# Narrower matmuls in the block solve of a hybrid layer's recurrence, and ten weight k-steps moved out of it

## The chip, the cores and the metric

The kernel runs on one core of one Trainium2 chip. The time is the device time of one execution in microseconds (us); of several runs the median is taken, and less is better. TensorE (PE in the profile) does the matmuls, and its weight loads have rows of their own (PEld). VectorE is DVE, ScalarE is ACT, GpSimd is POOL, SyncE is SP.

## The reference, cut to what matters

The layer is a chain of three blocks over 256 tokens. The change touches one branch of the first: a two-directional recurrence with 12 heads of 64 channels.

```python
def rwkv7_scan(r, w, k, v, kk, a):
    decay = jnp.exp(-jnp.exp(w))
    b = kk * a
    def step(S, inp):
        r_t, d_t, k_t, v_t, kk_t, b_t = inp
        sa = jnp.einsum('bhij,bhj->bhi', S, -kk_t)
        S = S * d_t[:, :, None, :] + sa[..., None] * b_t[:, :, None, :] + v_t[..., None] * k_t[:, :, None, :]
        return S, jnp.einsum('bhij,bhj->bhi', S, r_t)
...
    for d in range(N_DIR):
...
        if d == 0:
            y_sum = y_sum + rwkv7_scan(r4, wd4, kd4, v4, kk, ad4)
        else:
            y_sum = y_sum + flip(rwkv7_scan(flip(r4), flip(wd4), flip(kd4), flip(v4), flip(kk), flip(ad4)))
```

Everything around it (projections, attention, two more blocks with wide feed-forward products) is dense matmul over a stream of weights.

## The kernel before, in words

**Weights.** One stream of 563 weight tiles of 2048x128 passes through the core. Each tile is two units of 8 k-steps. SP fetches a unit into `raw`, ACT makes its high part (`split_hi`, L325, 128x1024), DVE its low part (`split_lo`, L334, 128x1024), and TensorE does three matmuls for each k-step (`product`, L345 to L347: high by high, high by low, low by high, 256 moving columns). The order of work on every engine is the order of the code; engines meet through counting semaphores (`need` waits for a named step of another engine, L199).

**The recurrence** is done in 4 chunks of 64 tokens (`NCH`, `CH`), for 6 pairs of heads (`PAIRS`), both directions `d` = 0 and 1 together. `pe_rwkv` is written out for the 6 pairs; on the other engines a pair is one round of a loop. Each pair has on TensorE: projections and a transpose, three groups of products of the chunk's keys (the grams: `mt`, `kat`, `m`, then `brt`, `krt`, `btok`, then `katv`, `krtv`, `ktok` and `u0_1`), a block solve in levels, and four steps through the chunks. A product is 8 matmuls of 64x64 by 64 columns (4 chunks, 2 heads); in float32 each has two records in the trace. Direction 1 crosses the heads (`cross`), so that the two directions use different quarters of the array, and `both` takes two products in turns.

**The levels** invert a triangular matrix per chunk: at level `l` (1 to 5) blocks of 2^l rows are joined in twos. For each direction, `level_x` multiplies `tm` by the masked matrix `ml[l]` into a bank, ACT copies the result to `x` (L1211), `level_t` and `level_u` multiply it with `u`, and DVE adds the banks to `tm` (L1292) and `u` (L1300). `tm` and `u` are the inverse and its transpose. TensorE takes the directions half a level apart: in one half step it does a double group (one direction's X, the other's T) and a single group (a U). All matmuls, copies and additions work on all 64 columns of each chunk.

**Weight k-steps among it.** Beside each pair 4 weight tiles are multiplied, 64 k-steps. `go(n)` puts the next n of them into TensorE's order: `GO_START` 2, `GO_PREP` 25, `GO_GRAM` 5, 4 and 6 behind the three grams, 10 among the levels (`GO_LEVEL`, two at first and one in each half step behind it), `GO_SOLVED` 2 behind the solve, and one (`GO_STEP`) at each of ten places of the chunk steps. The splits of later units stand in the levels too: on DVE `split_lo` behind the T addition of direction 1 in levels 1, 2 and 4, and a gate at level 3; on ACT `split_hi` behind levels 1 and 3. POOL makes `ml[l]` (L1152, L1163) and `u` from `mt` while the levels run.

Of the kernel before, what the change touches and what calls it, by code (L numbers as in the profile page):

```python
# [17 lines left out]
P = 128  # L18
D = 2048
KT = D // P  # L20
T = 256
# [70 lines left out]
GO_START, GO_PREP, GO_LEVEL, GO_SOLVED, GO_STEP = 2, 25, 1, 2, 1  # L92
GO_GRAM = (5, 4, 6)
# [157 lines left out]
def build(nc, stream, consts, params, w2, a2, wgu, memT, xT, metaT, out):  # L251
# [4 lines left out]
    with ctx:  # L256
# [721 lines left out]
        for d in range(2):  # L978
            o = B + 82 * K + 20 * K * d
            w = {}  # L980

            for k, n in enumerate(("abd", "rbd", "bbd", "kbd", "mt", "tm", "brt", "btok", "ktok", "nkatv", "kat", "krt", "u", "x")):
# [49 lines left out]
        def dve_kk(v, u):  # L1032
# [7 lines left out]
            elif u == A_T + X_T - 1:  # L1040
                kk_v.done(nc.vector.tensor_scalar(hw_sb[:], par[:, PCOL["w0"]:PCOL["w0"] + 24], 0.5, None, ALU.mult), "half")
                need(v, kk_v, "inv2")
                for b in THIRDS:
                    for p in (2 * b, 2 * b + 1):
# [7 lines left out]
                     + [f"{n}{d}" for d in D2 for n in (("t1_", "ml1_", "u0_", "u1_") if d == 0 else ("t1_", "ml1_"))]  # L1052
                     + [f"ml2_{d}" for d in D2] + ["u1_1"] + [f"ml{l}_{d}" for l in LV if l > 2 for d in D2])
# [75 lines left out]

        def chunk_of(d, s):  # L1130
            return s if d == 0 else NCH - 1 - s

        def pool_rwkv(pool):
# [4 lines left out]
            with pool.Fori(0, PAIRS) as p:  # L1138
# [8 lines left out]
                ident = four(const("istack"))  # L1147
                for d, w in enumerate(dirs):

                    need(pool, rw_v, f"m{d}", p)  # L1150
                    rw_o.done(nc.gpsimd.tensor_tensor(w["tm"][:], w["tm"][:], ident, ALU.add), f"t1_{d}")
                    rw_o.done(nc.gpsimd.tensor_tensor(w["ml"][1][:], w["mt"][:], level(1), ALU.mult), f"ml1_{d}")  # L1152
                    if d == 0:
                        rw_o.done(nc.gpsimd.tensor_tensor(w["u"][:], w["mt"][:], level(0), ALU.mult), f"u0_{d}")
                        need(pool, rw_o, f"u0_{d}", p)
                        rw_o.done(nc.gpsimd.tensor_tensor(w["u"][:], w["u"][:], ident, ALU.add), f"u1_{d}")
                for l in LV:
                    if l > 1:
                        for d, w in enumerate(dirs):
                            if l == 2 and d == 0:  # L1160

                                need(pool, rw_v, "q", p)
                            rw_o.done(nc.gpsimd.tensor_tensor(w["ml"][l][:], w["mt"][:], level(l), ALU.mult), f"ml{l}_{d}")  # L1163
                    if l == 2:
# [8 lines left out]
        def act_rwkv(act):  # L1173
# [3 lines left out]
            with act.Fori(0, PAIRS) as p:  # L1177
# [47 lines left out]
        def dve_rwkv(v):  # L1225
# [4 lines left out]
            with v.Fori(0, PAIRS) as p:  # L1230
# [57 lines left out]
                for l in LV:  # L1288
                    for d, w in enumerate(dirs):
                        if l < LEVELS - 1:  # L1290
                            need(v, rw_p, f"T{l}_{d}", p)
                            rw_v.done(nc.vector.tensor_tensor(w["tm"][:], w["tm"][:], value_part(bank_of(d, 0), 0), ALU.add), f"T{l}_{d}")  # L1292
# [7 lines left out]
                        rw_v.done(nc.vector.tensor_tensor(w["u"][:], w["u"][:], value_part(bank_of(d, 2), 0), ALU.add), f"U{l}_{d}")  # L1300
# [38 lines left out]
        def pe_rwkv(pe):  # L1339
# [3 lines left out]
            for p in range(PAIRS):  # L1343
# [68 lines left out]
                def level_x(l, d):  # L1412
# [8 lines left out]
                    return bank_of(d, 1), 0, w["ml"][l], w["tm"], d, f"X{l}_{d}"  # L1421
# [11 lines left out]
                def level_t(l, d):  # L1433
                    level_known(l, d)
                    return bank_of(d, 0), 0, dirs[d]["u"], dirs[d]["x"], d, f"T{l}_{d}"

                def level_u(l, d):
                    level_known(l, d)
                    return bank_of(d, 2), 0, dirs[d]["x"], dirs[d]["u"], 0, f"U{l}_{d}"

                for l in LV:
# [5 lines left out]
                    go(2 * GO_LEVEL if l == 1 else GO_LEVEL)  # L1447
# [5 lines left out]
                    if l < LEVELS - 1:  # L1453
                        go(GO_LEVEL)
                both(level_u(LEVELS - 1, 1))
                go(GO_SOLVED)
                for s in ST:
# [39 lines left out]
                    go(GO_STEP if s < NCH - 1 else BESIDE * KT - GO_START - GO_PREP - sum(GO_GRAM) - 2 * (LEVELS - 1) * GO_LEVEL - GO_SOLVED - (3 * NCH - 2) * GO_STEP)  # L1497
# [1866 lines left out]
```

How the kernel before makes its waits and increments, by code:

```python
def need(eng, steps, name, it=None):  # L197
    eng.wait_ge(steps.sem, steps.at(name, it))
# [88 lines left out]
        def folded(v, phase, tile, bank):  # L288
            nc.vector.tensor_reduce(fold[tile.parity][:], bank[:].rearrange("p (a t) -> p t a", a=2), AX.X, ALU.add).then_inc(fold_out, 1)
            v.wait_ge(fold_out, tile.local(1, fold_done(phase, 1)))
            return fold[tile.parity][:]
# [5 lines left out]
        def halves_added(v, phase, tile, ins, dst, bank, out_sem):  # L298
            ins.then_inc(half_out, 1)
            v.wait_ge(half_out, tile.local(1, 1 + sum(COUNT[q] for q in HALVED[:HALVED.index(phase)])))
            nc.vector.tensor_tensor(dst, dst, bank[:, T:], ALU.add).then_inc(out_sem, 1)
# [12 lines left out]
        def split_hi(act, tile, units=(0, 1)):  # L315
            if not tile.loops and tile.first + tile.t >= N_TILES + PAD:
                return
            for k in units:
                slot = (2 * tile.parity + k) % RING
                g = tile.first + tile.t
                act.wait_ge(raw_in[slot], tile.sum(16 * (g // 2 + 1), 8))
                if not tile.start:
                    act.wait_ge(units_used, tile.units(k + 1 - RING))
                nc.scalar.activation(w_hi[:, slot], raw[:, slot], ACT.Copy).then_inc(hi_ready, 1)
# [1 line left out]
        def split_lo(v, tile, units=(0, 1)):  # L327
# [3 lines left out]
            for k in units:  # L331
                slot = (2 * tile.parity + k) % RING
                v.wait_ge(hi_ready, tile.units(k + 1))
                nc.vector.tensor_tensor(w_lo[:, slot], raw[:, slot], w_hi[:, slot].bitcast(F),
```

## Time and profile before

| | |
|---|---|
| median of 3 runs | 3526.99 us |
| lowest and highest | 3524.95 and 3529.78 us |
| the profiled execution, its own time | 3526.12 us |
| its span in the trace | 3524.0 us |
| mean granted TensorE clock | 0.995 of full speed |
| instructions in the trace | 75021 |

The span runs from the first to the last instruction of the profiled execution; its own time is 2.12 us more. In the views below, a matmul's row begins where it enters the array and its length is modelled, and rows of successive matmuls overlap: how fast they follow each other is read from the starts. "x16" is 16 records merged.

### The profile page before, as it was taken

Reading aid. Unit: us, or ns where it says so; the run is one execution under the profiler, and the core shown is the slowest. Engines: PE = TensorE matmul, PEld = TensorE weight load, DVE = VectorE, ACT = ScalarE, POOL = GpSimd, SP = SyncE. Lnnn points to the kernel's source line nnn. Section 1 sums busy time; section 2 is a strip of 40 time slices with the busy share of each in tenths; the row PEclk is TensorE's granted clock in tenths of the full one; section 3 lists DMA queues with packets and bytes.
Section 4 is the critical chain, followed back from the end, with each engine's and each line's share of the span. In section 5 each row is a group of like instructions: output and inputs, shape, how many; then the busy total and the mean of one; then the engine's idle time right before and its main releaser. Section 6 shows DMA issues by size and latency. Waiting matters only on the chain.

```text
span 3524.0 us, 75021 instructions
## 1 busy us (share of the span) xinstructions
PE 3456.2 (98%) x27870; PEld 3151.2 (89%) x27870; DVE 2423.2 (69%) x3490; ACT 1642.0 (47%) x2248; POOL 289.4 (8%) x358
## 2 busy tenths in 40 slices
PE   8999999999999999999999999999999999999998
PEld 8999888899988899999888888888899988888886
DVE  6986777755676677976756565677766865656566
ACT  6456334444444434754444444444444644434344
POOL 5000234200020000002000000020000200000002
PEclk9999999999999999999999999999999999999999
DMA  7444222255655555555565555555554555555564
GB/s 253 160 156 144 86 86 86 82 171 179 204 191 188 184 178 175 168 169 181 185 194 181 194 185 193 182 188 191 174 161 162 173 185 185 191 185 194 181 194 140
DMA packets 164985, 604.04 MB, mean 171 GB/s; under 512 B 18336, under 2 KB 18464, under 8 KB 164560
## 3 DMA queue, kind: packets, MB, share of 16 engines
q1 hardware_dynamic: 163584, 596.16, 51.8%
q8 instruction: 135, 2.21, 0.3%
q10 hardware_dynamic: 1040, 3.16, 0.2%
q0 software_dynamic: 192, 2.23, 0.2%
q14 instruction: 34, 0.28, 0.0%
HBM read 599.38 MB, written 2.10 MB: 171 GB/s over the span
## 4 chain that ended last, share of the span: by engine, by line
PE 90%; DVE 6%; ACT 2%; issue 1%; POOL 0%; DMA 0%; ACTq 0%; DVEq 0%; POOLq 0%
PE bank L366 35%; PE bank L369 18%; PE bank L345 11%; PE bank L346 10%; PE bank L347 10%; PE bank L1349 4%; DVE w_lo L334 2%; ACT w_hi L325 1%; POOL x_norm_acc L466 0%; DVE nrm_kk L1039 0%; DVE X L2900 0%; PE bank L848 0%; DVE X L2904 0%; PE bank L731 0%; DVE conv_sq L2584 0%
## 5 line engine op out<-in xcount | busy, mean ns | idle before, releaser
L325 ACT ACTIVATE w_hi<-raw 128x1024 fp32r<-128x1024 f32 x1126 | 1157.6, 1053 | 827.2 <-PE bank L369 510.5
L334 DVE TENSOR_TENSOR w_lo<-raw,w_hi 128x1024 fp32r<-128x1024 f32 x1126 | 1350.0, 1236 | 99.9 <-ACT w_hi L325 99.6
L366 PE MATMUL bank<-hid,w_hi 128*128 128x512 f32 x2048 | 643.4, 395 | 0.0
L366 PE MATMUL bank<-u,w_hi 128*128 128x512 f32 x1536 | 484.4, 397 | 0.0
L345 PE MATMUL bank<-hx,w_hi 128*128 128x256 f32 x1568 | 466.1, 297 | 12.1 <-DVE w_lo L334 12.1
L369 PEld LDWEIGHTS bank<-hid,w_lo 128*128 128x128 f32 x2048 | 384.7, 188 | 90.9
L346 PE MATMUL bank<-hx,w_hi 128*128 128x256 f32 x1568 | 445.3, 284 | 0.0
L347 PE MATMUL bank<-hx,w_lo 128*128 128x256 f32 x1568 | 444.9, 284 | 0.3 <-issue 0.3
L366 PE MATMUL bank<-xh,w_hi 128*128 128x512 f32 x1312 | 413.5, 397 | 2.7 <-DVE w_lo L334 2.7
L369 PE MATMUL bank<-hid,w_lo 128*128 128x256 f32 x2048 | 402.3, 278 | 0.0
L369 PEld LDWEIGHTS bank<-u,w_lo 128*128 128x128 f32 x1536 | 289.5, 189 | 69.2
L345 PEld LDWEIGHTS bank<-hx,w_hi 128*128 128x128 f32 x1568 | 302.1, 193 | 27.6 <-issue 16.8
L366 PEld LDWEIGHTS bank<-hid,w_hi 128*128 128x128 f32 x2048 | 311.8, 189 | 0.1
L346 PEld LDWEIGHTS bank<-hx,w_hi 128*128 128x128 f32 x1568 | 302.7, 193 | 1.0 <-issue 1.0
L369 PE MATMUL bank<-u,w_lo 128*128 128x256 f32 x1536 | 302.4, 278 | 0.0
L347 PEld LDWEIGHTS bank<-hx,w_lo 128*128 128x128 f32 x1568 | 302.3, 193 | 0.0
L369 PEld LDWEIGHTS bank<-xh,w_lo 128*128 128x128 f32 x1312 | 247.2, 188 | 58.5
L369 PE MATMUL bank<-xh,w_lo 128*128 128x256 f32 x1312 | 258.4, 278 | 0.0
L366 PEld LDWEIGHTS bank<-u,w_hi 128*128 128x128 f32 x1536 | 234.1, 188 | 0.1
L2308 DVE SCALAR_TENSOR_TENSOR X<-X,bank 128x256 f32 (+1 forms) x128 | 54.0, 422 | 256.6 <-PE bank L369 256.2
L345 PE MATMUL bank<-u,w_hi 128*128 128x272 f32 (+1 forms) x768 | 220.7, 287 | 6.0 <-DVE w_lo L334 6.0
L346 PE MATMUL bank<-u,w_hi 128*128 128x272 f32 (+1 forms) x768 | 220.7, 287 | 0.0
(477 smaller groups left out, 5559.3 us busy)
## 6 DMA issues: line engine op xcount, KB each, us to landing
raw<-stream SPq DMA_DIRECT2D x1126, 512.0 KB, 4.0
x_raw<-xT SPq DMA_DIRECT2D x4, 512.0 KB, 7.5
mem_raw<-memT ACTq DMA_DIRECT2D x4, 512.0 KB, 9.5
x_res<-xT POOLq DMA_DIRECT2D x1, 2048.0 KB, 9.7
out<-X SPq DMA_DIRECT2D x3, 512.0 KB, 2.7
cst<-consts SPq DMA_DIRECT2D x1, 1504.0 KB, 13.6
out<-X SPq DMA_DIRECT2D x2, 256.0 KB, 2.2
w_sb<-w ACTq DMA_DIRECT2D x1, 384.0 KB, 4.8
```

What stands on the lines that cost most here:

```text
L325: nc.scalar.activation(w_hi[:, slot], raw[:, slot], ACT.Copy).then_inc(hi_ready, 1)
L334: nc.vector.tensor_tensor(w_lo[:, slot], raw[:, slot], w_hi[:, slot].bitcast(F), ALU.subtract).then_inc(lo_ready, 1)
L345: nc.tensor.matmul(dst, w_hi[:, slot, j], hi, start=first, stop=False)
L346: nc.tensor.matmul(dst, w_hi[:, slot, j], lo, start=False, stop=False)
L347: return nc.tensor.matmul(dst, w_lo[:, slot, j], hi, start=False, stop=last)
L366: nc.tensor.matmul(bank[:], w_hi[:, slot, i], both(moving, kt), start=kt == 0, stop=False)
L369: last = nc.tensor.matmul(bank[:, T:], w_lo[:, slot, i], moving[:, kt, 0, moving.shape[-1] - T:], start=False, stop=kt == KT - 1)
L1349: last = nc.tensor.matmul(out[halves()[r ^ cross]], lhs[halves()[r]], rhs[halves()[r]], start=start, stop=stop)
L2308: nc.vector.scalar_tensor_tensor(self.x[:, m], self.x[:, m], self.scale if self.is_group(g, 0) else 1.0, banks[tile.parity][:, 0:T], ALU.m ...
```

## The change

Joining two blocks of 2^l rows changes only half of the columns. The changed kernel works on that half alone.

- `with_bit(ap, l, bit)` picks the columns whose number has bit l equal to `bit`: 32 of each chunk's 64, in runs of 2^l.
- X and T take and write the half with bit l equal to d, U the other half. Each of these matmuls has 32 moving columns in place of 64. What is loaded as weights (`ml[l]`, `u`, `x`) keeps its 64 columns, and so the number of matmuls and of loads stays.
- The copy on ACT and the two additions on DVE handle 128 elements a partition in place of 256.
- Since X serves as weights in full, its other half must be zero: POOL sets it, one memset for each level and direction (10 a pair), and each level has an `x` of its own, laid over tiles that are no longer needed (`kat`, `krt`, `kbd`, `bbd`). POOL waits for TensorE's `u0_1` before level 2, and ACT for the memset before each copy. ACT's wait for the U product of the level before is gone.
- The ten weight k-steps among the levels go: four more stand behind the second gram (`GO_GRAM` 5, 8, 8), two more behind the third, four more behind the solve (`GO_SOLVED` 6).

```diff
-GO_START, GO_PREP, GO_LEVEL, GO_SOLVED, GO_STEP = 2, 25, 1, 2, 1
-GO_GRAM = (5, 4, 6)
+GO_START, GO_PREP, GO_SOLVED, GO_STEP = 2, 25, 6, 1
+GO_GRAM = (5, 8, 8)
...
+            w["x"] = {l: at(f"x{l}_{d}", o + K * k, [P, NCH, CH]) for l, k in enumerate((13, 10, 11, 3, 2), 1)}
...
+        def with_bit(ap, l, bit):
+
+            if len(ap.shape) == 3:
+                ap = ap.rearrange("p c i -> p (c i)")
+            return ap.rearrange("p (g b t) -> p g b t", b=2, t=1 << l)[:, :, bit]
...
+                def rest_zero(l, d):
+                    rw_o.done(nc.gpsimd.memset(with_bit(dirs[d]["x"][l][:], l, 1 - d), 0.0), f"x{l}_{d}")
...
                             if l == 2 and d == 0:
 
                                 need(pool, rw_v, "q", p)
+                                need(pool, rw_p, "u0_1", p)
...
-                        if l > 1:
-
-                            need(act, rw_p, f"U{l - 1}_{d}", p)
-                        rw_a.done(nc.scalar.activation(w["x"][:], value_part(bank_of(d, 1), 0), ACT.Copy), f"X{l}_{d}")
+                        need(act, rw_o, f"x{l}_{d}", p)
+                        rw_a.done(nc.scalar.activation(with_bit(w["x"][l][:], l, d), with_bit(bank_of(d, 1)[:, 0:T], l, d), ACT.Copy), f"X{l}_{d}")
...
-                            rw_v.done(nc.vector.tensor_tensor(w["tm"][:], w["tm"][:], value_part(bank_of(d, 0), 0), ALU.add), f"T{l}_{d}")
+                            rw_v.done(nc.vector.tensor_tensor(with_bit(w["tm"][:], l, d), with_bit(w["tm"][:], l, d), with_bit(bank_of(d, 0)[:, 0:T], l, d), ALU.add), f"T{l}_{d}")
...
-                        rw_v.done(nc.vector.tensor_tensor(w["u"][:], w["u"][:], value_part(bank_of(d, 2), 0), ALU.add), f"U{l}_{d}")
+                        rw_v.done(nc.vector.tensor_tensor(with_bit(w["u"][:], l, 1 - d), with_bit(w["u"][:], l, 1 - d), with_bit(bank_of(d, 2)[:, 0:T], l, 1 - d), ALU.add), f"U{l}_{d}")
...
-                        for bank, o, lhs, rhs, cross, name in products:
-                            last = heads2(bank[:, o + CH * c:o + CH * c + CH], lhs[:, c], rhs if rhs is istack else rhs[:, c], cross=cross)
+                        for bank, o, lhs, rhs, cross, name, *columns in products:
+                            dst, moving = bank[:, o + CH * c:o + CH * c + CH], rhs if rhs is istack else rhs[:, c]
+                            if columns:
+                                dst, moving = with_bit(dst, *columns), with_bit(moving, *columns)
+                            last = heads2(dst, lhs[:, c], moving, cross=cross)
...
-                    go(2 * GO_LEVEL if l == 1 else GO_LEVEL)
...
-                    if l < LEVELS - 1:
-                        go(GO_LEVEL)
```

TensorE's order in one half step of the levels, the X of level 2 in direction 1 with the T of direction 0 there, in the kernel before. A name behind the comma is the weights, the one ahead of it the moving operand; the number behind `u` or `x` tells the directions apart (126 and 127 are direction 0).

```order
L345 MATMUL bank<-hx,w_hi 128x256
L346 MATMUL bank<-hx,w_hi 128x256
L347 MATMUL bank<-hx,w_lo 128x256
L1349 MATMUL bank<-x_127,u_126 64x64 x2
L1349 MATMUL bank<-tm_144,ml_1_154 64x64 x2
...
L1349 MATMUL bank<-u_126,x_127 64x64 x8
L345 MATMUL bank<-hx,w_hi 128x256
L346 MATMUL bank<-hx,w_hi 128x256
L347 MATMUL bank<-hx,w_lo 128x256
```

The same half step in the changed kernel, from the single group ahead of it to the double group behind it.

```order
L1361 MATMUL bank<-u_155,x_1_156 64x16x2 x8
L1361 MATMUL bank<-x_0_128,u_126 64x8x4 x2
L1361 MATMUL bank<-tm_148,ml_1_162 64x8x4 x2
...
L1361 MATMUL bank<-u_126,x_0_128 64x8x4 x8
L1361 MATMUL bank<-tm_119,ml_0_134 64x4x8 x2
L1361 MATMUL bank<-x_1_157,u_155 64x8x4 x2
```

The two rows of a double group come four times in turns. The weight k-step on either side is gone, and each matmul moves 8 runs of 4 columns in place of 64 columns; the groups, their order and their number are the same.

POOL's order from the second `tm` on in the kernel before, up to level 3.

```order
L1151 TENSOR_TENSOR tm_144<-tm_144,cst 128x256 [waits rwkv_dve]
L1152 TENSOR_TENSOR ml_1_153<-mt_143,cst 128x256
L1163 TENSOR_TENSOR ml_0_129<-mt_118,cst 128x256 [waits rwkv_dve]
L1163 TENSOR_TENSOR ml_1_154<-mt_143,cst 128x256
L1167 TENSOR_TENSOR u_151<-u_151,cst 128x256 [waits rwkv_dve]
L1163 TENSOR_TENSOR ml_0_130<-mt_118,cst 128x256
L1163 TENSOR_TENSOR ml_1_155<-mt_143,cst 128x256
```

The same stretch in the changed kernel.

```order
L1162 TENSOR_TENSOR tm_148<-tm_148,cst 128x256 [waits rwkv_dve]
L1163 TENSOR_TENSOR ml_1_161<-mt_147,cst 128x256
L1158 MEMSET x_1_156 128x64x2
L1176 TENSOR_TENSOR ml_0_133<-mt_118,cst 128x256 [waits rwkv_pe]
L1158 MEMSET x_0_128 128x32x4
L1176 TENSOR_TENSOR ml_1_162<-mt_147,cst 128x256
L1158 MEMSET x_1_157 128x32x4
L1181 TENSOR_TENSOR u_155<-u_155,cst 128x256 [waits rwkv_dve]
L1176 TENSOR_TENSOR ml_0_134<-mt_118,cst 128x256
L1158 MEMSET x_0_129 128x16x8
```

A memset of half an `x` stands behind each `ml`, and level 2 waits for TensorE as well.

## Rows read from the trace of the kernel before

**Rows 1.** The page: busy shares, granted clock in 40 slices, chain that ended last.

```profile
PE 3456.2 (98%) x27870; PEld 3151.2 (89%) x27870; DVE 2423.2 (69%) x3490; ACT 1642.0 (47%) x2248; POOL 289.4 (8%) x358
PEclk9999999999999999999999999999999999999999
PE 90%; DVE 6%; ACT 2%; issue 1%; POOL 0%; DMA 0%; ACTq 0%; DVEq 0%; POOLq 0%
```

**Rows 2.** Chain of pair 2's levels, in time: start us, us, what.

```profile
502.17 0.61 PE bank L1349 x16
502.78 0.32 PE bank L345
503.10 0.12 PE bank L346
...
503.69 1.08 PE bank L1349 x48
504.77 0.32 PE bank L345
...
505.32 1.08 PE bank L1349 x48
...
515.08 1.08 PE bank L1349 x48
...
516.70 0.64 PE bank L1349 x19
517.44 0.39 ACT x L1211
517.88 0.68 PE bank L1349 x16
518.56 0.32 PE bank L345
```

**Rows 3.** Timeline in pair 1's levels: start us, us, engine, instruction [idle before, releaser].

```profile
457.22 0.42 DVE L1292 TENSOR_TENSOR tm<-tm,bank 128x256 f32<-128x256 f32 x1 [0.70 <-PE bank L1349]
457.56 1.22 DVE L334 TENSOR_TENSOR w_lo<-raw,w_hi 128x1024 fp32r<-128x1024 f32 x1
458.06 0.27 PE L1349 MATMUL bank<-x,u 64*64 64x64 f32 x2
458.69 0.41 DVE L1300 TENSOR_TENSOR u<-u,bank 128x256 f32<-128x256 f32 x1
458.93 0.39 ACT L1211 ACTIVATE x<-bank 128x256 f32<-128x256 f32 x1 [1.30 <-PE bank L1349]
459.02 0.42 DVE L1292 TENSOR_TENSOR tm<-tm,bank 128x256 f32<-128x256 f32 x1
459.21 1.05 ACT L325 ACTIVATE w_hi<-raw 128x1024 fp32r<-128x1024 f32 x1
```

**Rows 4.** Timeline: float32 products with 128-column weights, 128 and 64 moving columns.

```profile
2590.51 1.95 PE L2713 MATMUL bank<-qd,ki 128*128 128x128 f32 x16
2592.21 0.36 PE L345 MATMUL bank<-xh,w_hi 128*128 128x256 f32 x1
...
2623.65 0.78 PE L2748 MATMUL bank<-qd,gla_state 128*128 128x64 f32 x6
2624.26 0.66 PE L2746 MATMUL bank<-gla_ps,v_tok 128*128 128x128 f32 x4
```

**Rows 5.** Groups by form: shapes xcount | busy us, mean ns | idle before.

```profile
L1211 ACT ACTIVATE x<-bank 128x256 f32<-128x256 f32 x20 | 7.7, 385 | 26.6 <-PE bank L1349 26.6
L1220 ACT ACTIVATE sas<-bank 128x64 f32<-128x64 f32 x24 | 4.5, 224 | 30.6 <-PE bank L1349 30.6
L1332 DVE TENSOR_TENSOR kkn<-kkn,bank 128x128 f32 x9 | 2.6, 285 | 5.4 <-PE bank L1349 5.4
L437 POOL MEMSET x_norm_acc<- 128x256 f32 x1 | 0.3, 312 | 0.3 <-POOLq L3357 0.3
```

**Rows 6.** POOL's timeline in pair 1, third gram and levels.

```profile
450.67 1.64 POOL L1167 TENSOR_TENSOR u<-u,cst 128x256 f32<-128x256 f32 x1 [0.55 <-DVE u L1285]
452.27 5.22 POOL L1163 TENSOR_TENSOR ml<-mt,cst 128x256 f32<-128x256 f32 x6
```

**Rows 7.** Waits, 360 to 700 us: us in total, times, longest.

```profile
PEld bank L1349 <- issue: 7.0, 12, 1.7
PE bank L1349 <- issue: 4.1, 4, 1.6
PEld bank L1349 <- POOL ml L1163: 1.1, 3, 0.6
```

More of the change, by code:

```diff
@@ L980, in build @@
             w = {}
-            for k, n in enumerate(("abd", "rbd", "bbd", "kbd", "mt", "tm", "brt", "btok", "ktok", "nkatv", "kat", "krt", "u", "x")):
+            for k, n in enumerate(("abd", "rbd", "bbd", "kbd", "mt", "tm", "brt", "btok", "ktok", "nkatv", "kat", "krt", "u")):
                 w[n] = at(f"{n}{d}", o + K * k, [P, NCH, CH])
+            w["x"] = {l: at(f"x{l}_{d}", o + K * k, [P, NCH, CH]) for l, k in enumerate((13, 10, 11, 3, 2), 1)}
             w["ml"] = {l: at(f"ml{l}_{d}", o + 13 * K + K * l, [P, NCH, CH]) for l in range(1, LEVELS)}
@@ L1051, in build @@
         rw_o = Steps(sem("rwkv_pool"), ["w2t", "a2t", "vbd"] + [f"{n}{d}" for d in D2 for n in ("kbd", "rbd")]
-                     + [f"{n}{d}" for d in D2 for n in (("t1_", "ml1_", "u0_", "u1_") if d == 0 else ("t1_", "ml1_"))]
-                     + [f"ml2_{d}" for d in D2] + ["u1_1"] + [f"ml{l}_{d}" for l in LV if l > 2 for d in D2])
+                     + [f"{n}{d}" for d in D2 for n in (("t1_", "ml1_", "x1_", "u0_", "u1_") if d == 0 else ("t1_", "ml1_", "x1_"))]
+                     + [f"{n}2_{d}" for d in D2 for n in ("ml", "x")] + ["u1_1"]
+                     + [f"{n}{l}_{d}" for l in LV if l > 2 for d in D2 for n in ("ml", "x")])
         rw_v = Steps(sem("rwkv_dve"), [f"{n}{d}" for d in D2 for n in ("u", "s")] + [f"{n}{d}" for d in D2 for n in ("ad", "bb", "t", "kd")]
@@ L1152, in pool_rwkv @@
                     rw_o.done(nc.gpsimd.tensor_tensor(w["ml"][1][:], w["mt"][:], level(1), ALU.mult), f"ml1_{d}")
+                    rest_zero(1, d)
                     if d == 0:
@@ L1162, in pool_rwkv @@
                                 need(pool, rw_v, "q", p)
+                                need(pool, rw_p, "u0_1", p)
                             rw_o.done(nc.gpsimd.tensor_tensor(w["ml"][l][:], w["mt"][:], level(l), ALU.mult), f"ml{l}_{d}")
+                            rest_zero(l, d)
                     if l == 2:
@@ L1420, in level_x @@
                         need(pe, rw_v, f"T{l - 1}_{d}", p)
-                    return bank_of(d, 1), 0, w["ml"][l], w["tm"], d, f"X{l}_{d}"
+                    return bank_of(d, 1), 0, w["ml"][l], w["tm"], d, f"X{l}_{d}", l, d
                 def level_known(l, d):
@@ L1434, in level_t @@
                     level_known(l, d)
-                    return bank_of(d, 0), 0, dirs[d]["u"], dirs[d]["x"], d, f"T{l}_{d}"
+                    return bank_of(d, 0), 0, dirs[d]["u"], dirs[d]["x"][l], d, f"T{l}_{d}", l, d
                 def level_u(l, d):
                     level_known(l, d)
-                    return bank_of(d, 2), 0, dirs[d]["x"], dirs[d]["u"], 0, f"U{l}_{d}"
+                    return bank_of(d, 2), 0, dirs[d]["x"][l], dirs[d]["u"], 0, f"U{l}_{d}", l, 1 - d
                 for l in LV:
@@ L1496, in pe_rwkv @@
                         rw_p.done(last1, f"Y{s}_1")
-                    go(GO_STEP if s < NCH - 1 else BESIDE * KT - GO_START - GO_PREP - sum(GO_GRAM) - 2 * (LEVELS - 1) * GO_LEVEL - GO_SOLVED - (3 * NCH - 2) * GO_STEP)
+                    go(GO_STEP if s < NCH - 1 else BESIDE * KT - GO_START - GO_PREP - sum(GO_GRAM) - GO_SOLVED - (3 * NCH - 2) * GO_STEP)
         yhl = [at(f"yhl{k}", B + o * K, [P, n, 2, T], R) for k, (o, n) in enumerate(((74, 8), (54, 6), (128, 2)))]
```

## The prediction

> **What bounds the kernel now.** The page first: TensorE is busy for 98% of the span, the chain that ended last runs 90% over it, and its clock is full in all 40 slices [rows 1]. So a change counts only for what it does to the length of TensorE's order. Then the chain of waits within the levels. The ten half steps of pair 2 are read from it [rows 2]: X of level 1 (0.61 us), two k-steps, and from 503.69 eight half steps to 516.70, 1.63 us each: 1.08 of small matmuls (48 records: a double and a single group) and 0.55 of one k-step. Of this 0.55, the first matmul takes 0.32 where the next takes 0.12, so a k-step costs 3 x 0.12 = 0.36 us and changing over to it and back 0.2. Only at the end does TensorE stand, for the last copy of X, 0.39 us on ACT. From 502.17 to 518.56 the levels take 16.39 us, and in this pair no other wait is in them.
>
> So the k-steps do not fill holes that a view shows; the holes appear when they are gone. The timeline tells how large. The double group that begins at 458.06 is followed by the copy on ACT at 458.93 (0.87 later); the one a half step earlier, at 458.06 - 1.63 = 456.43, by the T addition at 457.22 and by a copy, both about 0.80 later [rows 3]. From the end of such an operation to TensorE's start it is 0.05 us (517.44 + 0.39 to 517.88) [rows 2].
>
> **The moving columns.** The change halves what streams through the array and leaves what is loaded. Two rows with float32 weights of 128 columns tell what that is worth [rows 4]: with 128 moving columns 16 records follow in 1.70 us (2590.51 to 2592.21), 0.106 each; with 64 moving columns 6 follow in 0.61 us (2623.65 to 2624.26), 0.102 each. Half the columns saved 4%, so something that goes with the weights sets the pace there. In the levels, 1.08 us less some 0.14 for the first load and the change-over is 0.94, and since a double group uses the two other quarters of the array beside, it takes no longer than a single one: 0.47 each. A quarter has 8 records in that time, 0.058 apart, about half of 0.106 for half as many weight columns. I therefore take the groups as unshortened: 0 saved, but for the last record, whose stream ends some 0.03 us earlier. The other bound is a true halving, 0.23 us less in each group.
>
> The Trainium skill, "TensorE: Matmul & The Clock Gate", section "LDWEIGHTS (loading the stationary operand)", says that a load takes the weights' columns divided by 1.2 in ns; for 64 columns that is an estimate of 53 ns, for 128 of 107 ns, and the trace's 0.058 and 0.102 to 0.106 agree. By this rule the groups stay as long as they are; by the number of columns moved they would halve, which is the first rival below.
>
> **The copies and additions.** 128x64 on ACT takes 0.224 and 128x256 takes 0.385, so 128x128 is put at 0.28; on DVE 128x128 takes 0.285 in place of 0.42 [rows 3, 5]. If the short runs of columns cost as much as before, it is 0.39 and 0.42; the other bound is the 0.22 of 64 columns.
>
> **A half step without its k-step.** TensorE's work is about 0.98 + 0.05 for the first load. The chain is longer: 0.80 or 0.87 from the start of the double group to the operation behind it, less 0.03, then 0.285, then 0.05 to 0.06. This gives 1.12 and 1.18 in turns, 1.15 on average. TensorE waits about 0.1 us in each.
>
> **Splits that were covered.** DVE does a unit's split behind the T addition of direction 1 in levels 1, 2 and 4: addition at 457.22, split at 457.56, U addition at 458.69, the other direction's T addition at 459.02 [rows 3]. That is 1.80 after the first, where 1.63 + a little was asked, and TensorE did not notice. The starts are 0.34, 1.13 and 0.33 apart; with additions shorter by 0.13 the second comes 0.21 + 1.13 + 0.21 = 1.55 behind the first. It is wanted 1.12 + 0.70 - 0.76 = 1.06 behind it (0.76 and 0.70 from the start of the double group to a T addition: the product that stands first in the group is ready 0.06 earlier). Of the 0.49 the longer copy path of that half step (1.18 against 0.70 + 0.285 + 0.06) hides 0.13, and 0.36 us stays, twice (levels 1 and 2). At level 4 the last U waits for the delayed U addition, 0.23 us. On ACT the split behind levels 1 and 3 (1.05 [rows 3]) delays the next copy by 0.04 each.
>
> **The sum for one pair.** X of level 1 to the first double group 0.73 - 0.03 + 0.28 + 0.06 = 1.04; eight half steps 8 x 1.15 = 9.20; DVE's splits 0.72, ACT's 0.08; X of level 5 to the last U 1.18 - 0.03 - 0.11 = 1.04; the late addition 0.23; the last U with the change-over, 0.65. Together 12.96 us, against 16.39: 3.43 less. The ten k-steps come back at 0.36 between other k-steps, where no change-over is added: 3.57 to 3.6 us. Net +0.15 us a pair, +0.9 us for six. In short, the nine change-overs saved (1.8 us) and the double wait for copies become waits of the same size.
>
> **Moved work, queue by queue.** The first extra k-step behind the second gram belongs to the same weight tile as those before it; the 16th k-step of that tile is now done ahead of the levels, so ACT's two splits in the levels find their slot free at least as early. No DMA is issued by a moved instruction. SP waits for the splits on DVE, which keep their place in DVE's order. SP and ACT get no new wait but ACT's for a memset. The levels begin 6 x 0.36 = 2.1 us later, and the grams' products behind the second gram 1.4 us later. POOL's new wait for `u0_1` ends about 0.6 us after POOL came free before. It then has ten memsets more. 128x256 takes 0.31 [rows 5]; for 128x128 I take 0.2. POOL made the last six `ml` in 5.22 us from 452.27, 0.87 each [rows 6]. With the memsets a level costs POOL 2 x (0.87 + 0.2) = 2.1 us, where TensorE asks for one in 2.3, and POOL is about 2 us ahead at level 3. So nothing; with memsets at 0.31 it would be 2.4 a level, and the lead still covers the three levels. POOL's three waits at the levels' start (1.1 us in all [rows 7]) should go, up to -1.1.
>
> **Against the execution.** The sum is made against the profiled execution: span 3524.0 + 0.9 - 0.5 = 3524.4, and 2.1 around it gives 3526.5. The median of the runs was 0.9 above that execution's own time, so 3527.4; with a little more waiting for instructions (below) I say 3528.
>
> **The rivals.** A difference under 0.2% (7 us) can hardly be told from none here.
>
> Forecast, no change that counts: 3520 to 3534 us, chance 0.62.
>
> Rival 1, the narrower matmuls do go faster, down to half. For it: 64 moving columns, at the 0.106 that 128 took, need 0.053, also near the 0.058 between records of a quarter, so in the levels either could set the pace. Against it: the 4% above [rows 4]. Then a half step is 0.95 and 0.89, with 0.23 off each path, and TensorE's work 0.5; DVE's and ACT's splits cost 1.43 in all, since the half steps no longer cover them; term by term as above the levels are 0.81 + 7.36 + 1.43 + 0.81 + 0.44 + 0.40 = 11.25 us. That is 5.14 less, 1.57 net, 9.4 us for six: 3518 us. Chance 0.20; a case halfway falls within 0.2%.
>
> Rival 2, slower: TensorE runs out of instructions. It stood 11.1 us "for issue" at these matmuls [rows 7], in 16 waits of up to 1.7 us, at places that differ from pair to pair; in pair 2 there was none. A level section has 28 products x 16 records x 2 = 896 instructions and had 60 for k-steps: 58 a us before, 896 / 12.96 = 69 a us after. If waits come when instructions are used up faster than they arrive, 19% more demand in the section with most of them could double the total: +11 us, 3538. It decides the sign from 1.2 us more a pair. Against it: TensorE now has gaps of its own in each half step in which instructions can arrive. Chance 0.12.
>
> Rival 3, slower by a little: short runs of 2 or 4 columns make copies and additions as long as whole ones. Then 0.12 more a half step, 1.15 us a pair, +7 us: 3535. Against it: nothing here shows it either way. Chance 0.04. Other things 0.02.
>
> **The numbers.** Faster by over 0.2%: rival 1, 0.20. Slower: rivals 2 and 3 and half of the rest, 0.17. Same: 0.63. The range takes in rival 1 at its 3518 and rival 3, and leaves out rival 2 at its full size and what is faster than 3517, together some 0.2: 3517 to 3535.
>
> **What would show it.** In the trace after: record starts of one quarter 0.058 apart in the levels (0.03 would be rival 1); half steps of about 1.15 us, and about 1.5 behind the two splits on DVE; short waits of TensorE for `x` and `tm` in each half step, several us in sum over the pairs, where there were 6; about 13 us from the first X to the change-over behind the last U. `issue` near 11 us (20 is rival 2). ACT's copy at 0.28 and DVE's addition at 0.285 (0.39 and 0.42 is rival 3). No wait of ACT or TensorE for POOL's memsets. The forecast is wrong if a half step is under 1.0 or over 1.3 us.

## The result and the profile after

The changed kernel takes 3550.93 us (median of 4 runs, 3549.06 to 3551.38), the kernel before 3526.88 us in the same comparison (4 runs, 3524.95 to 3529.78). The ratio is 1.007, with a 95% interval from 1.0058 to 1.0082: slower by 24 us, or 0.7%. The forecast was no change that counts, 3528 us in a range of 3517 to 3535, so it was wrong and the range too.

The page of the changed kernel, the rows that answer to [rows 1]:

```profile
PE 3468.1 (98%) x27870; PEld 3170.3 (89%) x27870; DVE 2408.7 (68%) x3490; ACT 1635.5 (46%) x2248; POOL 294.4 (8%) x418
PEclk9999989899999999999999999999999999999999
PE 88%; DVE 7%; ACT 2%; issue 2%; POOL 0%; DMA 0%; ACTq 0%; DVEq 0%; POOLq 0%
```

Two things are new. The granted clock is under nine tenths in two of the four slices that hold most of the recurrence (360 to 730 us), and in the chain the share of waits for nothing that the profile shows ("issue") went from 1 to 2%. The profiled execution's own time is 3549.06 us, its span 3547.3, its mean clock 0.987 of full speed, where it was 0.995. A digit of 9 in these rows stands for 90% or more, so a short stretch at half clock does not show in them.

The chain of waits in pair 2's levels shows both (start us, us, what; it answers to [rows 2]; pairs are counted from 0):

```profile
510.35 0.61 PE bank L1361 x16
...
511.06 0.29 ACT x L1223
...
511.39 1.12 PE bank L1361 x48
512.52 0.21 issue
512.73 0.73 PE bank L1361 x32
...
513.68 0.26 DVE w_lo L334
...
514.82 0.28 DVE u L1312
515.10 0.21 DVE tm L1304
515.30 0.09 issue
515.39 0.73 PE bank L1361 x32
...
518.07 1.12 PE bank L1361 x48
519.25 1.12 PE bank L1361 x48
...
520.93 1.81 issue
522.74 3.73 PE bank L1361 x88
526.47 0.51 PE bank L345
526.98 0.21 PE bank L346
```

X of level 1 takes 0.61 us as before and a double and a single group 1.12 where they took 1.08: half the moving columns did not shorten them. At 520.93 TensorE stands for 1.81 us and no engine holds it up. From 523.2 on TensorE's work takes about twice as long, the weight k-step's matmuls 0.21 us each where they take 0.12. The trace's windows tell the same of pairs 2 and 3 (window, its length, busy time and records of each engine, then the granted clock, the DMA engines' share and GB/s):

```profile
510.40:523.20 12.80, 9.15 (x386) 8.37 (x387) 6.00 (x17) 4.12 (x10) 6.05 (x13) 0.99 0.38 125
523.20:530.00 6.80, 6.80 (x89) 6.61 (x86) 2.20 (x5) 0.56 (x2) 0.87 (x3) 0.51 0.25 80
566.20:574.40 8.20, 6.60 (x273) 5.97 (x273) 4.70 (x12) 3.17 (x8) 6.02 (x13) 0.99 0.41 130
574.40:588.10 13.70, 12.17 (x215) 11.54 (x210) 3.68 (x10) 1.67 (x7) 0.87 (x3) 0.51 0.25 80
```

A clock of 0.5 is the lower of TensorE's two levels, 1.2 GHz. In each of the six pairs it begins 6 to 13 us after the first X and lasts 6.8 or 13.7 us, 68 us in all. In the kernel before no level section had any; its own stretches at half clock, beside the longer one at the program's end, lie elsewhere: 3.4 us from 360.2, from 373.8, and from two places behind the recurrence, and 6.8 us from 698.1.

Waits of the changed kernel, 360 to 700 us (in total, times, longest), beside [rows 7]:

```profile
PEld bank L1361 <- issue: 18.1, 36, 1.9
PE bank L1361 <- issue: 8.8, 14, 1.8
PE bank L1361 <- ACT x L1223: 3.5, 9, 0.5
PE bank L1361 <- DVE tm L1304: 3.3, 9, 0.4
```

Its groups by form, beside [rows 5]:

```profile
L1223 ACT ACTIVATE x<-bank 128x128 f32<-128x128 f32 x60 | 16.7, 279 | 80.9 <-PE bank L1361 75.3 <-POOL ml L1176 5.4
L1304 DVE TENSOR_TENSOR tm<-tm,bank 128x128 f32<-128x128 f32 x48 | 13.7, 286 | 36.9 <-PE bank L1361 36.9
L1158 POOL MEMSET x<- 128x128 f32 x60 | 12.4, 207 | 0.0
```

The operations cost what was reckoned (0.28, 0.285, 0.2). The waits for issue are 26.9 us where they were 11.1; these sums add the idle time of TensorE's two rows, loads and matmuls, so one pause can stand in them twice.

### The profile page after: what moved, and what is told of

Read it like the earlier page. It is cut to its first block, busy times and chain, and to the rows that moved or that the text cites. A ratio compares the mean times of both kernels' runs of the same rounds, so it can differ in the third digit from the quotient of the medians.

```text
span 3547.3 us, 75099 instructions
## 1 busy us (share of the span) xinstructions
PE 3468.1 (98%) x27870; PEld 3170.3 (89%) x27870; DVE 2408.7 (68%) x3490; ACT 1635.5 (46%) x2248; POOL 294.4 (8%) x418
## 3 DMA queue, kind: packets, MB, share of 16 engines
q8 instruction: 135, 2.21, 0.3%
## 4 chain that ended last, share of the span: by engine, by line
PE 88%; DVE 7%; ACT 2%; issue 2%; POOL 0%; DMA 0%; ACTq 0%; DVEq 0%; POOLq 0%
PE bank L366 34%; PE bank L369 17%; PE bank L345 11%; PE bank L346 10%; PE bank L347 10%; PE bank L1361 4%; DVE w_lo L334 3%; ACT w_hi L325 1%; POOL x_norm_acc L466 0%; DVE nrm_kk L1040 0%; DVE X L2912 0%; PE bank L848 0%; DVE X L2916 0%; PE bank L731 0%; DVE conv_sq L2596 0%
## 5 line engine op out<-in xcount | busy, mean ns | idle before, releaser
L345 PE MATMUL bank<-hx,w_hi 128*128 128x256 f32 x1568 | 464.1, 296 | 12.6 <-DVE w_lo L334 12.6
L345 PEld LDWEIGHTS bank<-hx,w_hi 128*128 128x128 f32 x1568 | 305.8, 195 | 24.1 <-issue 17.0
L346 PEld LDWEIGHTS bank<-hx,w_hi 128*128 128x128 f32 x1568 | 306.3, 195 | 1.0 <-issue 1.0
## 6 DMA issues: line engine op xcount, KB each, us to landing
cst<-consts SPq DMA_DIRECT2D x1, 1504.0 KB, 13.4
```

Source lines behind the costliest of these rows:

```text
L345: nc.tensor.matmul(dst, w_hi[:, slot, j], hi, start=first, stop=False)
L346: nc.tensor.matmul(dst, w_hi[:, slot, j], lo, start=False, stop=False)
```

## Experiments

Three theories stood after the result, each for a part of the 24 us or all of it. **Instructions:** with the k-steps gone, TensorE runs out of instructions oftener (rival 2). **Clock:** with 32 moving columns the granted clock falls, and what follows is done at half speed. **Half steps:** they are simply longer than the sum had them. The runs were made in four sets; each time stands beside the kernel before on the same chip.

### Narrow matmuls and moved k-steps, each alone

`e1_narrow_old_places` is the changed kernel with the ten k-steps back among the levels.

```diff
+GO_START, GO_PREP, GO_LEVEL, GO_SOLVED, GO_STEP = 2, 25, 1, 2, 1
+GO_GRAM = (5, 4, 6)
...
+                    go(2 * GO_LEVEL if l == 1 else GO_LEVEL)
```

> Half the columns in matmuls, copies and additions, the ten weight k-steps back among the levels as before. Theory A (the granted clock falls because the levels alone, narrower and with gaps, leave the array too little to do): full-width k-steps every half step keep the clock full, so mean clock 0.995, no half-clock stretch in the levels, and 3522 to 3528 us, since the groups keep their length (records of a quarter 0.058 apart). Theory B (narrow columns alone make the clock fall): half-clock stretches remain, 3540 us or more. Theory C (waits for instructions are the loss): issue at these matmuls back from 27 to about 11 us.

Measured 3537.86 us against 3525.9, ratio 1.0028 (1.0015 to 1.0041). Its ten runs spread from 3523.27 to 3543.79 and follow the clock, as in these four: 3523.27 at 0.996, 3528.02 at 0.994, 3531.09 at 0.991, 3543.79 at 0.987. In the profiled one (0.988) the clock was at half in three pairs, for 13.7 us from 406.6 and from 468.1 us and for 30.7 us from 676.3. The waits for issue are 12.4 us, near the 11.1 of the kernel before. So narrow matmuls alone cost nothing that can be told in the run with the clock up, and it doesn't always stay up.

`e2_wide_new_places` is the kernel before with only the k-steps moved.

```diff
-GO_START, GO_PREP, GO_LEVEL, GO_SOLVED, GO_STEP = 2, 25, 1, 2, 1
-GO_GRAM = (5, 4, 6)
+GO_START, GO_PREP, GO_LEVEL, GO_SOLVED, GO_STEP = 2, 25, 0, 6, 1
+GO_GRAM = (5, 8, 8)
```

> All 64 columns everywhere as in the kernel before, only the ten k-steps moved (grams 5, 8, 8, six behind the solve). Theory A' (it is the missing k-steps that let the clock fall): half-clock stretches as in the changed kernel, 3545 to 3555 us. Theory B (narrow columns needed): clock 0.995, half steps of about 1.3 us (0.13 more for copy or addition than with half the elements), levels some 14 us, total 3527 to 3535. Theory C (instructions): issue near 20 us at full clock and 3535 to 3545.

Measured 3544.2 against 3525.9, ratio 1.0053 (1.0036 to 1.007), at a clock of 0.994. Moving the k-steps costs 18 us when copies and additions stay whole. The clock is at half for 6.8 us from the end of one pair's levels on and for 3.4 us in another's, so the clock is a small part of it at most; the waits for issue are 31.6 us.

`e3_wide_matmul_half_copies` is the changed kernel with 64 moving columns in the levels' matmuls.

```diff
-                            if columns:
-                                dst, moving = with_bit(dst, *columns), with_bit(moving, *columns)
```

> The changed kernel, but the level matmuls move all 64 columns again; copies and additions stay at half, k-steps stay moved. The extra columns hit the zero half or are not read. Theory B (narrow columns let the clock fall): clock 0.995 again and about the 3528 that the prediction had, 3520 to 3532. Theory A' (missing k-steps): as the changed kernel, 3545 to 3555 with half-clock stretches. Theory C: clock full but issue still 20 us or more.

Measured 3539.18 against 3525.9, ratio 1.0039 (1.0025 to 1.0053), clock 0.995. Streaming twice the columns makes the changed kernel 11 us faster. With the clock nearly always full it still loses 13 us: half clock lasts 3.4 us in the levels of three pairs. Here TensorE's waits for issue are 42.5 us (11.1 before), and ten breaks of over 0.9 us from one matmul's start to the next in the levels, 15.9 us in all, end with no releaser. Before there were three in the levels and one ahead of pair 4's, 5.0 us in all. The longest, in the chain of pair 3 of this kernel:

```profile
572.06 0.80 PE bank L1361 x36
572.86 2.80 issue
575.66 3.42 PE bank L1361 x59
```

### What the breaks are

Instructions reach the core over a DMA queue of their own, which the page lists as "q8 instruction: 135, 2.21": 135 packets, 2.21 MB, so 16 KB each. I set the landing of these packets beside the breaks (worked out from the traces' start and duration of each packet, us; a break runs from one matmul's start to the next):

```
kernel   break from, to      length   last packet landed   from there to the end
before   463.28 to 464.33     1.05        462.97                 1.37
before   601.84 to 603.71     1.86        602.24                 1.47
after    520.71 to 522.74     2.03        521.33                 1.41
after    576.69 to 578.51     1.82        576.99                 1.52
e3       464.19 to 466.25     2.06        464.86                 1.39
e3       572.64 to 575.66     3.02        574.11                 1.55
```

All 20 breaks of over 0.9 us with no releaser in before (4), the changed kernel (6) and e3 (10) end 1.23 to 1.56 us after a landing, while packets land only every 4 to 5 us there. I read this so: TensorE has used up what it had, and resumes about 1.4 us after the next packet is in. To try this, the number of instructions must change while the work stays.

`e5_fewer_instructions` is e3 with three quarters of the U matmuls left out, so no block inverse is computed.

```diff
+                            if columns and name[0] == "U" and c < NCH - 1:
+                                continue
...
-                        rw_v.done(nc.vector.tensor_tensor(with_bit(w["u"][:], l, 1 - d), with_bit(w["u"][:], l, 1 - d), with_bit(bank_of(d, 2)[:, 0:T], l, 1 - d), ALU.add), f"U{l}_{d}")
+                        rw_v.done(nc.vector.tensor_tensor(with_bit(w["u"][:], l, 1 - d), with_bit(w["u"][:], l, 1 - d), with_bit(w["u"][:], l, 1 - d), ALU.max), f"U{l}_{d}")
```

> e3_wide_matmul_half_copies with three quarters of the matmuls of the U products left out (only the last chunk is multiplied), and DVE's U addition replaced by a maximum of u with itself of the same size: the block inverse is incomplete. 72 small records in place of 96 in each half step, on an order that waits for the copies anyway. Theory C (instructions arrive too slowly, 256 at a time, and a landing frees TensorE 1.3 to 1.5 us later): a batch lasts 4.5 us in place of 3.3, the waits of 1 to 3 us go, issue falls from 42 to some 15 us, levels 13.5 to 14.5 us a pair, 3522 to 3528 us if the clock stays full. Rival (the waits are made by something else, and the levels are bound by the chain alone): one to three waits over 0.9 us a pair remain and the time is over 3535 us. With less work on the array the clock may fall; then the levels' first part, at full clock, is compared.

Measured 3546.21 against 3525.65, ratio 1.0058 (1.0043 to 1.0073). No break of over 0.9 us without a releaser was left, and yet it was slower than e3. Its clock was 0.985: at half in all six pairs, for 10.2 or 13.7 us, as in this window of the first pair.

```profile
404.00:417.60 13.60, 10.85 (x216) 9.78 (x217) 6.72 (x18) 2.61 (x7) 1.77 (x6) 0.50 0.36 119
```

Taking matmuls away changed two things at once, and by the new maximum a third, below, so this run decides nothing on the time that instructions cost. It shows that the clock can fall with 64 moving columns as well, when there are fewer matmuls.

`e7_wide_u_few_instructions` keeps the columns: a U is 2 matmuls of 256 columns for 8 of 64.

```diff
+                            if columns and name[0] == "U":
+                                if c == NCH - 1:
+                                    rw_p.done(heads2(bank[:, 0:T], lhs[:, 0], rhs[:].rearrange("p c i -> p (c i)")), name)
+                                continue
```

> The kernel of e3 (half copies, level matmuls of 64 moving columns, k-steps moved away), but each product for U in a level is 2 matmuls of 256 moving columns in the place of 8 of 64: the same columns stream for the same time, from a quarter of the instructions. The products take the first chunk's weights for all chunks and VectorE's addition for U takes u twice, so the block inverse isn't computed; all else is timed as it was. If e3's levels are long because TensorE runs out of instructions, the waits over 0.9 us that end without a releaser go, the idle time of PE and PEld with the releaser issue falls from 42.5 us to 15 or less in the levels, the levels of a pair take 13.4 to 13.9 us instead of 16.4, the granted clock stays at 0.995, and the time is that of the forecast, 3524 to 3530. If the instruction supply is not the cause, the time stays at 3535 to 3542.

Measured 3532.08 against 3526.46, ratio 1.0016 (1.0007 to 1.0025), clock 0.994. It has the same number of instructions as e5 (73659 in the trace), the same operations on the other engines, and only more columns to stream: by the differences to the kernel before it is 15 us faster than e5. The levels take 13.9 to 14.4 us in four pairs (first X to last U record; 16.4 on average in e3; 13.4 to 13.9 was expected), and of the ten breaks two are left, 1.16 and 1.73 us. "Issue" fell less than expected, from 42.5 to 22.5 us, since short stretches of it stand in every half step (what they are is told below). The time missed the expected 3524 to 3530 by 2 us. In one pair the clock fell all the same, for 6.8 us, and the trace shows a tax of my own edit: VectorE's `max(u, u)` runs in SBUF alone and takes up to 0.82 us while POOL works beside it, 0.28 to 0.29 while POOL is idle.

```profile
455.33 1.66 POOL L1176 TENSOR_TENSOR ml<-mt,cst 128x256 f32<-128x256 f32 x1
456.32 0.82 DVE L1312 TENSOR_TENSOR u<-u 128x128 f32<-128x128 f32 x1
```

`e8_wide_u_old_places` has the same edit with the k-steps at their old places.

> The kernel of e4 (half copies, level matmuls of 64 moving columns, k-steps at their old places) with the same edit for U as e7: 2 matmuls of 256 moving columns for 8 of 64, first chunk's weights, u added to itself, so the block inverse isn't computed. The kernel before waits for instructions in its levels too (11.1 us in rows 7). If those waits lie on the path, the time falls by up to 5 us from e4's 3524.2, to 3518 to 3522. If they are covered by other waits, it stays at 3523 to 3526.

Measured 3518.34 against 3526.46, ratio 0.998 (0.9971 to 0.9989), as expected, with no break of over 0.9 us in the levels.

### The same without the tax

`e10_wide_u_added_from_bank` is e7 with an addition that reads the bank.

```diff
-                        rw_v.done(nc.vector.tensor_tensor(with_bit(w["u"][:], l, 1 - d), with_bit(w["u"][:], l, 1 - d), with_bit(w["u"][:], l, 1 - d), ALU.max), f"U{l}_{d}")
+                        rw_v.done(nc.vector.scalar_tensor_tensor(with_bit(w["u"][:], l, 1 - d), with_bit(bank_of(d, 2)[:, 0:T], l, 1 - d), 0.0, with_bit(w["u"][:], l, 1 - d), ALU.mult, ALU.add), f"U{l}_{d}")
```

> The kernel of e7 (half copies, 64 moving columns, k-steps moved away, U products as 2 matmuls of 256 columns, no block inverse), but VectorE's step for U is bank x 0 + u, which reads the PSUM bank as the changed kernel's addition does. In e7 the step max(u, u) read and wrote SBUF alone and took 0.53 to 0.82 us beside POOL's work, where the addition from the bank takes 0.28. If that was e7's own tax, the fourth double group begins 5.2 us after the first one's X and not 5.73, each pair is about 0.5 us shorter, and the time is 3532.1 less 3, 3529. If the tax is not on the path, 3532.

Measured 3527.92 against 3524.91, ratio 1.0009 (0.9999 to 1.0019), clock 0.995. The tax was real, 2.6 us: 5.6 over the kernel before in e7, 3.0 here. Its half steps begin where those of e3 begin, to 0.01 us, up to the first break that e3 has, so it is e3 with a better supply: e3's 13.3 us over before are 3.0 here. The waits for issue are 28.3 us all the same, so that sum alone doesn't tell a want of instructions.

`e12_wide_u_old_places_bank` is e8 with this addition.

> The kernel of e8 (half copies, 64 moving columns, k-steps at their old places, U products as 2 matmuls of 256 columns, no block inverse) with the step bank x 0 + u. In e8 the k-steps cover the longer step, so it stays at 3518 within 2 us. Against e10 only the places of the ten k-steps differ, with no want of instructions and at full clock in both: the difference is what moving them costs by itself, 6 x 0.15 = 1 us by the forecast, and 8 us or more if the half steps without k-steps are longer than forecast.

Measured 3516.49 against 3524.91, ratio 0.9976 (0.9966 to 0.9985), clock 0.995. Against e10 only the places of ten k-steps differ: 11.4 us. That is above the 8 that was named for longer half steps.

### The clock by itself

`e9_narrow_u_few_instructions` is the changed kernel with U as 2 matmuls of 128 moving columns and `max(u, u)`, so e7 with half the columns.

> The changed kernel (half copies, level matmuls of 32 moving columns, k-steps moved away) with each product for U as 2 matmuls of 128 moving columns in the place of 8 of 32: as many columns as in the changed kernel, a quarter of the instructions, first chunk's weights and u added to itself, so the block inverse isn't computed. This leaves the clock alone without the waits for instructions. If the fall of the granted clock to half costs time by itself, the clock stays at 0.99 or below, the product after the levels takes over 3.5 us to start, and the time is 3536 to 3542. If the clock plays no part, it is e7's, 3524 to 3530.

Measured 3546.14 against 3526.46, ratio 1.0056 (1.004 to 1.0071), clock 0.985, half clock in all six pairs. It is 14.1 us over e7; the expected 3536 to 3542 lacked the tax.

`e11_narrow_u_added_from_bank` is the same with the addition from the bank.

> The kernel of e9 (as the changed kernel with 32 moving columns, U products as 2 matmuls of 128 columns, no block inverse) with the step bank x 0 + u in the place of max(u, u). Against e10 only the moving columns of the levels differ, and neither is short of instructions. If the clock alone costs what after and e3 differ by (11.7 us), it is e10 + 12, some 3541, with half-clock stretches in all six pairs. If e9's 14 us over e7 were a matter of the longer steps on SBUF, the two are nearer than 6 us.

Measured 3540.48 against 3524.91, ratio 1.0043 (1.0028 to 1.0057), clock 0.988, half clock in five of six pairs. The sixth, pair 1, has the same levels at full clock as e10, 13.63 us against 13.65 from the first X to the last U record; the others take 15.0 to 16.2. From one pair's first X to the next one's it is 52.07 us there against 52.19 in e10, and 55.1 to 56.6 in the other four that have a next. Breaks of 0.95 and 2.03 us stand in two of them, as two do in e10. So half the columns cost 12.6 us (e11 less e10), and where the clock stays up they cost nothing.

### Fewer k-steps moved

`e4_half_copies_old_places` is e3 with all k-steps at their old places, `e6_five_ksteps_kept` is e3 with five of them in the levels, whose edit begins so:

```diff
-GO_START, GO_PREP, GO_SOLVED, GO_STEP = 2, 25, 6, 1
-GO_GRAM = (5, 8, 8)
+GO_START, GO_PREP, GO_LEVEL, GO_SOLVED, GO_STEP = 2, 25, 1, 4, 1
+GO_GRAM = (5, 6, 7)
```

> Half the elements in copies and additions, all 64 columns in the matmuls, k-steps among the levels as in the kernel before. In every half step TensorE's own order (1.63 us) is longer than the chain through the copy, so only the two waits for the last copy (0.1 us each) get shorter: 1 to 2 us less than before, 3524 to 3526 us, clock 0.995 or more. If shorter copies shorten the half steps themselves, 3515 us or less.

> e3_wide_matmul_half_copies with five of the ten k-steps kept in the levels, one in each half step that has DVE's split. Theory C: a batch of 256 instructions lasts 3.7 us, between the 4.1 of the kernel before and the 3.3 of e3, and DVE's splits are covered again; issue between 11 and 42 us and the time between 3526 and 3539: 3528 to 3534 us. If the waits have nothing to do with the rate, about 3539 less what the covered splits give (4 us): 3535 us or more.

Measured against 3525.65: e4 3524.19, ratio 0.9996 (0.9987 to 1.0005), clock 0.997; e6 3532.42, ratio 1.0018 (1.0009 to 1.0028). Half copies at the old places are worth nothing that can be told. With five k-steps moved the loss is 6.8 us, between e4's -1.5 and e3's +13.3. No kernel that computes the whole reference beat the one before; e8 and e12 do, but leave out the block inverse.

## Why the prediction was wrong

Differences to the kernel before, each from its own set, in us (copies and additions at half but in the first row):

| levels | k-steps at old places | k-steps moved |
|---|---|---|
| 64 moving columns, all instructions, whole copies and additions | 0 (the kernel before) | +18.3 (e2) |
| 64 moving columns, all instructions | -1.5 (e4) | +13.3 (e3) |
| 64 moving columns, U in 2 matmuls | -8.4 (e12) | +3.0 (e10) |
| 32 moving columns, U in 2 matmuls | | +15.6 (e11) |
| 32 moving columns, all instructions | +12.0 (e1, wide spread) | +24.0 (the changed kernel) |

The 24.0 us are, along one way through the table, -1.5 for the smaller copies and additions (e4), +14.8 for the moved k-steps (e4 to e3), and +10.7 for the clock (e3 to the changed kernel). The middle one has two parts, below. Another way round it is -1.5 (e4), +13.5 for narrow matmuls with the k-steps in their old places (e4 to e1) and +12.0 for the moved k-steps (e1 to the changed kernel).

**Right: the groups are not shortened.** 0.61 us for X of level 1 as before, 1.12 for a double and a single group where it was 1.08, with half the columns. A group is 0.03 us shorter, as was put down: 16 records of X start within 0.436 us, 0.463 in e3. Rival 1 fell. The copies, additions and memsets cost what was put down. POOL made nobody late that the trace shows.

**Right: the splits.** Two half steps around a split were reckoned at 1.12 + 1.18 + 0.36 + 0.04 = 2.70 us. The chain of e10's pair 1 has 2.70 twice:

```profile
449.09 0.64 PE bank L1361 x16
...
449.83 0.29 ACT x L1223
...
450.16 1.12 PE bank L1361 x36
451.28 0.24 issue
451.52 0.76 PE bank L1361 x32
...
454.22 0.76 PE bank L1361 x32
...
456.92 1.12 PE bank L1361 x36
458.03 0.10 issue
458.13 0.45 PE bank L1361 x13
458.58 0.07 issue
458.64 0.58 PE bank L1361 x19
...
459.32 0.28 ACT x L1223
459.61 0.25 issue
459.85 0.76 PE bank L1361 x32
...
462.40 0.65 PE bank L1361 x4
463.05 0.32 PE bank L345
```

**Wrong in size: "a half step without its k-step".** From 451.52 to 454.22 and to 456.92 it is 2.70 each. But the half step from 450.16 took 1.36 and that from 456.92 1.21, where 1.12 to 1.18 was said. The step that failed is the hand-over, "from the end of such an operation to TensorE's start it is 0.05 us". That holds for the last copy, where the weight load itself waits: the copy ends at 517.82, the load starts at 517.88 [rows 2]. In the half steps 0.10 to 0.25 us of "issue" come between. The trace of e10 shows what stands there: TensorE's wait instructions (`need`, L199), which aren't counted busy and are in no view above. The copy in the half step from 450.16 ends at 451.31. The wait for it ends at 451.36, a second wait, for VectorE's additions, runs from 451.41 to 451.46, the load starts at 451.49 and the first matmul at 451.52: 0.21 us. Behind the copy that ends at 459.60 two such waits run one after the other, and it is 0.25 us.

From the first X to the change-over behind the last U pair 1 takes 13.96 us (449.09 to 463.05), with one short pause at 458.6, which ends 1.41 us after a landing. Pair 0, which has none, takes 13.84, where the prediction had 12.96 and the kernel before 16.39. So the levels give back 2.55 us and not 3.43; the ten k-steps return at 3.6 as reckoned (the levels begin 2.16 us later, and the first chunk step 1.43 us later behind the last U, e10 against e12). Net +1.05 us a pair and not +0.15: 6.3 us for six in place of 0.9. The hand-overs are the part of the 0.88 us over the sum that the trace names; it isn't split further.

**Wrong in weight: rival 2, TensorE runs out of instructions.** It was named, with its mechanism and its price (+11 us), and got 0.12. The reason against it, "TensorE now has gaps of its own in each half step in which instructions can arrive", is what failed. Ten breaks in e3's levels against three before show that these gaps don't save it; with a quarter of the instructions for U they are two, of 1.71 and 1.46 us (e10). My reading is that a level section with fewer us uses a packet up sooner, while the next one lands no earlier for it; that was argued from the landings, and no run changed the arrival of packets. Of the 14.8 us for the moved k-steps (e4 to e3) 7.0 are the longer half steps, by the same working from e4's 16.28 us in place of 16.39. The remaining 7.8 are put down to this and to the 3.4 us at half clock in three pairs, so the price was somewhat too high and the chance far too low. The kernel before pays for the same thing, by e4 to e12 6.9 us; of that some 2 are shorter groups (levels of 15.80 against 16.13 us, six times), the rest is put down to pauses, of which e4 has two of over 0.9 us and e12 none.

**Missing: the clock.** The prediction read "its clock is full in all 40 slices" as a fact of the kernel, and no case had it fall. The reading was wrong already, since a 9 says 90% or more and the mean was 0.995. The clock is the largest term that one cause explains, 10.7 to 12.6 us (e3 to the changed kernel, e10 to e11). These are pair 0's levels from the first X on, the first two rows from the changed kernel, the other two from e3:

```profile
397.40:403.70 6.30, 4.62 (x201) 4.24 (x201) 2.68 (x7) 2.06 (x5) 6.02 (x13) 0.99 0.34 113
403.70:414.00 10.30, 10.05 (x253) 9.78 (x251) 5.52 (x14) 2.61 (x7) 0.87 (x3) 0.50 0.26 92
```

```profile
398.70:405.00 6.30, 4.43 (x186) 3.94 (x189) 2.50 (x7) 2.07 (x5) 6.19 (x13) 1.00 0.35 96
405.00:415.30 10.30, 7.44 (x280) 6.53 (x272) 5.66 (x16) 2.61 (x7) 0.79 (x3) 1.00 0.38 117
```

In the first 6.3 us TensorE is 4.62 us busy in the changed kernel and 4.43 in e3, and then the clock falls in the one and stays in the other. The two kernels differ in 32 or 64 moving columns alone. With the k-steps moved, e3 and e10 (64 columns) have at most 3.4 us at half clock in a pair's levels, behind or at the end of a break of 1.46 to 3.02 us, and e7 has 6.8 us once. The changed kernel, e9 and e11 (32 columns), and e5 (64, but a quarter of the U matmuls) lose it for 6.8 to 17.1 us in five or six pairs. The k-steps with their 256 moving columns don't hold it up by themselves: with them back and 32 columns elsewhere (e1) it falls in three pairs of the profiled run, and the median is 13.5 us over e4's. Breaks don't explain it: in pairs 1, 3 and 5 of the changed kernel the clock falls before the pair's first break of over 0.9 us.

The Trainium skill, "TensorE: Matmul & The Clock Gate", section "A second HAM failure mode: psum-queue depth-cycling", tells of a kernel whose short idle times between groups make the clock go back and forth between its two levels. The trace agrees in that no wait of TensorE in the changed kernel's levels is over 1.9 us. But short waits alone don't tell the kernels apart, since e3 waits longer in all (42.5 us of issue against 26.9) and keeps its clock but for 3.4 us in three pairs.

What stays open: e10 still has breaks of 1.71 and 1.46 us, so its 11.4 us over e12 are not all longer half steps (13.84 against 16.11 us, so 1.33 a pair, 8.0); the rest fits those breaks but wasn't tried apart. What it is in the work of a level section that lets the clock fall isn't settled: only the edits that did it are known. Nor was the hand-over tried by itself, in a kernel with fewer wait instructions.

## What to carry to other kernels

In this kernel the dense work between small matmuls that wait for each other did two things. It covered the waits (7.0 us for six pairs), and it kept down the breaks that end "issue" (the other 7.8, in part argued). The clock was a third matter, and it came with the narrower matmuls. Before taking such cover away, look in the profile for breaks that end "issue", and give more of them a price and a fair chance. Look up the granted clock in windows and not by the page's tenths, and treat a full clock as something that the change may move. Price a hand-over from a place of the same kind: here a load that waits itself took 0.05 us, and one behind one or two wait instructions 0.10 to 0.25. Streaming half the columns per matmul saved 0.03 us a group here, since the records came no faster, and cost 10.7 us.

## What the runs showed of the hardware

- The granted clock fell to half after 6.3 us in which TensorE was busy 4.62 (pair 0 of the changed kernel) and after 12.8 us in which it was busy 9.15 (pair 2). It stayed down through 6.8 to 13.7 us in which TensorE was busy 89 to 100%.
- In float32 with 64 weight columns, matmuls of 32 and of 64 moving columns follow each other 0.058 us apart in a quarter of the array at full clock (the changed kernel and e3). At half clock it is 0.107 with 32.
- Instruction packets are 16 KB (135 of them, 2.21 MB); in 20 breaks of three kernels TensorE resumed 1.23 to 1.56 us after a landing.
- Behind the end of a copy a weight load that waits itself is 0.05 us later (517.82 to 517.88), and with a further wait instruction between them the first matmul starts 0.21 us later (451.31 to 451.52).
- An operation on VectorE of 128x128 with all operands in SBUF took up to 0.82 us beside POOL's work and 0.28 to 0.29 without it (e7). The addition from a bank took 0.28 to 0.29 in both (the changed kernel, e10).
